# Three edits at the seams of a fused decoder layer: x in row tiles, unsplit products in the first gate/up group, high parts first in the down stage

## The reference

```python
xn = rmsnorm(x, n1g)
z = xn @ w_in                       # 2048 -> conv group, mLSTM q, k, v, o, 8 gate columns
y = concat(conv_group(z), mlstm(z)) # short conv and chunked mLSTM, each with its own norm
x = x + y @ w_out
hn = rmsnorm(x, n2g)
x = x + (silu(hn @ wg) * (hn @ wu)) @ wd
y_out = rmsnorm(x, final_g)
```

## Time and profile before

| | |
|---|---|
| runs | 2497.23, 2492.79, 2495.88 us; median 2495.88 us |
| profiled execution | 2492.38 us, of which the span shown is 2490.3 us |
| PE busy | 2458.9 us (99%) |
| weight loads of PE | 2393.4 us (96%), beside the matmuls |
| DVE, ACT, POOL busy | 1771.7, 895.0, 38.4 us |
| DMA | 325.54 MB, mean 131 GB/s |
| last chain, by engine | PE 94%, DVE 3%, DMA 2%, ACT 1%, issue 1% |

### The profile page before, as it was taken

The page is one execution under the profiler, slowest core; times in us unless marked ns, Lnnn a source line. Parts: engine busy times, 40 slices in busy tenths (PEclk is TensorE's granted clock), DMA queues, the critical chain, the costliest instruction groups (busy, mean ns, idle before and its releaser), DMA issues.

```text
span 2490.3 us, 44310 instructions
## 1 busy us (share of the span) xinstructions
PE 2458.9 (99%) x17632; PEld 2393.4 (96%) x17632; DVE 1771.7 (71%) x2487; ACT 895.0 (36%) x1236; POOL 38.4 (2%) x60
## 2 busy tenths in 40 slices
PE   8999999999999998999999999999999999999998
PEld 8999999999999997999999999999999899999886
DVE  7576575575687668887778777877777866866435
ACT  5212222222133335434343434343444533544313
POOL 0000000000000000000000000000000000000100
PEclk9999999999999999999999999999999999999999
DMA  5433333333235665344343433434333655745722
GB/s 131 99 119 95 84 112 100 89 104 102 86 115 155 186 200 187 111 127 119 102 134 111 128 112 109 127 110 128 100 111 105 250 155 158 266 129 142 274 81 76
DMA packets 458922, 325.54 MB, mean 131 GB/s; under 512 B 14130, under 2 KB 429006, under 8 KB 456368
## 3 DMA queue, kind: packets, MB, share of 16 engines
q1 hardware_dynamic: 403704, 250.29, 34.6%
q10 hardware_dynamic: 51448, 58.42, 7.7%
q0 software_dynamic: 3584, 14.16, 1.5%
HBM read 264.49 MB, written 58.34 MB: 130 GB/s over the span
## 4 chain that ended last, share of the span: by engine, by line
PE 94%; DVE 3%; DMA 2%; ACT 1%; issue 1%; SPq 0%; DVEq 0%; ACTq 0%
PE ps L604 21%; PE ps L844 17%; PE ps L848 17%; PE ps L846 17%; PE ps L607 10%; PE ps L612 3%; PE ps L859 2%; PE ps L952 2%; PE ps L956 2%; PE ps L954 2%; DMA xtok<-in_x_sample_dram 1%; DMA opraw<-hop 0%; PE ps L960 0%; PE ps L961 0%; PE ps L871 0%
## 5 line engine op out<-in xcount | busy, mean ns | idle before, releaser
L844 PE MATMUL ps<-ophi,gw_ring 128*128 128x288 f32 x3248 | 963.2, 297 | 11.7 <-ACT p1c L1291 6.6
L846 PE MATMUL ps<-oplo,gw_ring 128*128 128x288 f32 x3248 | 959.1, 295 | 0.0
L848 PE MATMUL ps<-ophi,gw_ring 128*128 128x288 f32 x3248 | 957.2, 295 | 0.0
L844 PEld LDWEIGHTS ps<-ophi,gw_ring 128*128 128x128 f32 x3248 | 610.1, 188 | 13.6 <-ACT p1c L1291 7.0
L848 PEld LDWEIGHTS ps<-ophi,gw_ring 128*128 128x128 f32 x3248 | 612.7, 189 | 0.0
L846 PEld LDWEIGHTS ps<-oplo,gw_ring 128*128 128x128 f32 x3248 | 610.9, 188 | 0.2
L1017 ACT ACTIVATE whi<-wraw 128x512 fp32r<-128x512 f32 x256 | 160.7, 632 | 597.3 <-PE ps L607 418.5
L604 PE MATMUL ps<-xhi,whi 128*128 128x288 f32 x1536 | 332.6, 298 | 0.0
L607 PE MATMUL ps<-xhi,wlo 128*128 128x288 f32 x1536 | 328.8, 296 | 0.0
L604 PE MATMUL ps<-xlo,whi 128*128 128x288 f32 x1536 | 328.7, 296 | 0.0
L2100 DVE TENSOR_TENSOR gw_ring<-graw_a,gw_ring 128x1024 fp32r<-128x1024 f32 x195 | 238.7, 1224 | 113.4 <-ACT gw_ring L1264 112.8
(11 more groups left out here) (338 smaller groups left out, 2667.6 us busy)
## 6 DMA issues: line engine op xcount, KB each, us to landing
wraw<-in_w_in_dram SPq DMA_DIRECT2D x96, 512.0 KB, 3.9
graw_a<-in_w_ffn_gate_dram SPq DMA_DIRECT2D x59, 512.0 KB, 3.8
graw_a<-in_w_ffn_up_dram SPq DMA_DIRECT2D x59, 512.0 KB, 4.7
graw_a<-in_w_ffn_down_dram SPq DMA_DIRECT2D x42, 512.0 KB, 6.3
wraw<-in_w_out_dram SPq DMA_DIRECT2D x32, 512.0 KB, 4.3
opraw<-hop SPq DMA_DIRECT2D x14, 1152.0 KB, 11.4
graw_b<-in_w_ffn_gate_dram SPq DMA_DIRECT2D x29, 512.0 KB, 3.8
graw_b<-in_w_ffn_up_dram SPq DMA_DIRECT2D x29, 512.0 KB, 4.8
```

The costliest lines, as they stand in the source:

```text
L844: pe.matmul(out, gw_ring[:, slot, 0, k, :], ophi[p][:, k, :], start=start and k == 0, stop=False, skip_group_check=True)
L846: pe.matmul(out, gw_ring[:, slot, 0, k, :], oplo[p][:, k, :], start=False, stop=False, skip_group_check=True)
L848: mm = pe.matmul(out, gw_ring[:, slot, 1, k, :], ophi[p][:, k, :], start=False, stop=k == GK - 1, skip_group_check=True)
```

## The change

Three parts, with nothing else touched.

**x by tiles of tokens.** SP loads six tiles of 96 tokens with whole rows of 8 KB (seven DMAs in the place of fifteen; the last tile is 32 rows of the prompt and 64 of the sample). A unit of work is now half a token tile, n = 2 t + kh with 8 k tiles each: eight transposes, one ACT copy and one DVE subtraction of 768 elements, 12 units in the place of 16. The gate products of one token half run in one piece, the first behind unit 8, the second at the end. The sums of squares are one per tile (three on ACT, three on DVE) and stand behind the units. The first weight quarters are split at n = 5 and 7.

```diff
-    X_PIECES = ((0, 2), (2, 2), (4, 4), (8, 4), (12, 4))
+    XU = 2 * XT
+    KU = KT // 2
-    SQ_ACT = 4
-    IDLE_FIRST, IDLE_X, IDLE_PIECE = 6, 14, (2, 8)
+    SQ_ACT = 3
+    IDLE_FIRST, IDLE_X = 6, 10
...
+            for t in range(XT - 1):
+                sp.dma_start(xtok[:, t, :], xp[t * XTW:(t + 1) * XTW, :]).then_inc(tok_in[t], 16)
+            sp.dma_start(xtok[0:last, XT - 1, :], xp[TP - last:TP, :]).then_inc(tok_in[XT - 1], 16)
+            sp.dma_start(xtok[last:XTW, XT - 1, :], xs[:, :]).then_inc(tok_in[XT - 1], 16)
...
+            def gates(a):
+                pe.wait_ge(x_lo, XU // 2 * (a + 1))
+                for k in range(KT):
+                    for moving in (xhi, xlo):
...
+            for n in range(XU):
+                t, kh = n // 2, n % 2
+                if n >= 3:
+                    pe.wait_ge(x_lo, n - 2)
+                if kh == 0:
+                    pe.wait_ge(tok_in[t], 16 if t < XT - 1 else 32)
+                for i in range(KU):
+                    k = kh * KU + i
+                    mm = pe.transpose(ps[:, 2 + 2 * (n % 3) + i // 4, (i % 4) * XTW:(i % 4 + 1) * XTW],
...
+                if n == XU - 4:
+                    pe.wait_ge(gw_lo, 2)
+                    gates(0)
+            gates(1)
...
+            for n in range(XU):
+                src, own = unit(n)
+                dve.wait_ge(x_hi, n + 1)
+                tt(own(xlo), src, own(xhi).bitcast(F32), ALU.subtract).then_inc(x_lo, 1)
+                if n in (5, 7):
+                    split(1, n // 2 - 2, V_G1)
+            for t in range(SQ_ACT, XT):
+                ins = square(t)
```

```diff
+                    pe.wait_ge(g_lo, p + 1)
+                    pe.wait_ge(op_hi, p - 1)
+                    pe.wait_ge(tok_in[p - 2], 16 * 2)
+                    for k in range(GK):
+                        mm = pe.matmul(ps[:, bank, 0:HT], gw_whole[:, p % 3, 0, k, :], opraw[p][:, k, :],
+                                       start=start and k == 0, stop=k == GK - 1, skip_group_check=True)
+                    mm.then_inc(g_used, 1)
...
             def operand_low(j):
+                dve.wait_ge(g_used, j + 3)
+                dve.wait_ge(op_hi, 5 + 2 * j + 2)
+                for k0, k1 in ((0, 3), (3, 6), (6, GK)):
...
+            whole_ready(0, 0, 3)
+            weight_sum(0, 0, 4)
+            whole_ready(0, 0, 4)
+            norm_start()
+            whole_ready(0, 0, 5)
+            norm_end()
             operand_low(0)
+            upper_gate(0, 0)
+            whole_ready(0, 0, 6)
+            upper_up(0, 0)
             operand_low(1)
             operand_low(2)
             weight_sum(0, 1, 1)
-            group(0, 1, norm=(norm_start, norm_end))
+            group(0, 1, second=True)
```

```diff
+            def first_blocks():
+                pe.wait_ge(dh_hi, 1)
+                pe.wait_ge(d_hi, 1)
+                for part in range(3):
+                    if part == 1:
+                        pe.wait_ge(d_lo, 1)
+                    elif part == 2:
+                        pe.wait_ge(dh_lo, 1)
+                    h, w = (hlo if part == 2 else hhi)[0], (dwlo if part == 1 else dwhi)[0]
+                    for t in range(4):
+                        if part == 0 and t >= 2:
+                            pe.wait_ge((c11_ok, c12_ok)[t - 2], NG1)
...
-                for t in range(5):
+                for t in range(5) if n else (4,):
```

More of the change, by code:

```diff
@@ L320, in hybrid_trunk_step @@
         tile_read = sem("tile_read")
-        tok_in = [sem(f"tok_in{b}") for b in range(len(X_PIECES))]
+        tok_in = [sem(f"tok_in{b}") for b in range(XT)]
         g1_in, gw_in, small_in = sem("g1_in"), sem("gw_in"), sem("small_in")
@@ L876, in group @@
                 bank_a, bank_b, bank_c = BANK_A[u % 3], 1, 4
+                split = lambda p: pe.wait_ge(op_lo, 3 * (p - 2) + 3) if first and u == 1 else None
                 if first and u == 2:
@@ L963, in down_block @@
                 return mm
+            def first_blocks():
[10 more added lines that the diff above has]
+                            pe.wait_ge((c11_ok, c12_ok)[t - 2], NG1)
+                        for k in range(DK4):
+                            pe.matmul(ps[:, DOWN_BANK[t], :], h[:, k, t * P:(t + 1) * P], w[:, k, :],
+                                      start=part == 0 and k == 0, stop=False, skip_group_check=True)
+            first_blocks()
             for n in range(2 * NBD * NCD):
@@ L1024, in _, with square, unit @@
             act.activation(rstd_col[:, 0:1], ident[:, 0:1], ACT.Copy)
-            act.wait_ge(gw_g, 1)
+            act.wait_ge(gw_lo, 1)
             act.activation(gw[:, :, 0:2 * H], gw_raw[:], ACT.Copy).then_inc(gw_hi, 1)
[L1028 to L1042, removed]
-                if k in (KT - 4, KT - 2):
-                    q = (k - (KT - 4)) // 2
-                    hi(1, q, gain=q + 1)
-            for b, t in squares:
-                square(b, t)
+            def square(t):
+                x = xtok[:, t, :]
+                act.activation(x, x, ACT.Square, accum_out=ss_part[:, t, 0:1]).then_inc(ss_ok, 1)
+            def unit(n):
+                t, kh = n // 2, n % 2
+                cols = slice((t % 3) * XTW, (t % 3 + 1) * XTW)
+                own = lambda v: v.rearrange("p (h b k a) t -> p h b k a t", h=2, b=2, a=2)[:, kh, :, :, t // 3, cols]
+                bank = 2 + 2 * (n % 3)
+                return ps[:, bank:bank + 2, 0:4 * XTW].rearrange("p b (k t) -> p b k t", t=XTW), own
+            for n in range(XU):
+                src, own = unit(n)
+                act.wait_ge(xt_done, n + 1)
+                act.activation(own(xhi), src, ACT.Copy).then_inc(x_hi, 1)
+                if n in (5, 7):
+                    hi(1, n // 2 - 2, gain=n // 2 - 1)
+            for t in range(SQ_ACT):
+                square(t)
             hi(1, 2, gain=3)
@@ L1309, in h_store, with group @@
                     act.dma_start(h_t[g - 1 - FS], hf[:, (g - 1) % 2].rearrange("p a t -> p (a t)")).then_inc(hf_st, 16)
-            def group(m, u, first=False, root=False, last=False):
+            def group(m, u, first=False, last=False):
                 g = m * GU + u
@@ L1409, in _ @@
             act.wait_ge(w_used, 4 * I_FFN)
[L1410 removed]
+            for j in range(5):
+                operand_last(j)
+            keep_copy(0, 0, 0, p1c, 2, c11_ok, p1c_ok)
+            whole_copy(0, 0, 3)
+            keep_copy(0, 0, 1, p5c, 4, c22_ok, p5c_ok)
             operand_hi(0)
[L1412 to L1413 removed]
+            whole_copy(0, 0, 4)
             operand_hi(1)
[L1415 to L1417 removed]
+            keep_copy(0, 0, 2, u2c, 2, c12_ok, u2c_ok)
+            whole_copy(0, 0, 5)
             operand_hi(2)
[L1419 to L1420 removed]
+            whole_copy(0, 0, 6)
+            act.wait_ge(r2_in, 1)
+            act.activation(rstd[:], rstd[:], ACT.Sqrt).then_inc(r2_ok, 1)
             operand_hi(3)
[L1422 to L1424 removed]
             operand_hi(4)
[L1426 to L1427 removed]
+            group(0, 1, first=True)
             for w in range(2, GU):
@@ L2192, in pair_sum, with group @@
                 tt(out, a, b, ALU.subtract).then_inc(t_step, 1)
-            def group(m, u, norm=None):
+            def group(m, u, second=False):
                 g = m * GU + u
@@ L2202, in sums @@
                         pair_sum(m if u else m - 1, v, n)
-                upper_up(g - 1, v)
+                if not second:
+                    upper_up(g - 1, v)
                 product_low(m, u, 0)
```

166 lines of the change are left out of this document (52 added, 114 removed).

## The result

| | before | after |
|---|---|---|
| median of 8 runs each, us | 2493.57 | 2501.33 |
| lowest to highest | 2491.82 to 2497.23 | 2499.14 to 2504.22 |
| profiled execution, us | 2492.38 | 2500.83 |
| its span, us | 2490.3 | 2499.1 |

The ratio after/before is 1.003 with a 95% interval of 1.0019 to 1.0040: slower by 7.8 us, where 5.1 less was forecast. It lies outside the range (2485.3 to 2497.3), beyond even the slower rival (2498.3).

The account below looks back on a forecast made before the run. PE, busy 99% of the span, was taken as the bound, so gains come only where it stands still or does less. Terms +2.5 - 4.5 - 3.1 = -5.1 gave 2490.8 on the median, range 2485.3 to 2497.3.

Parts of the forecast that it names:

- Down's exit, -3.1: At the exit of down's block products PE's 3.08 us wait for `hs` goes: -3.1 us, bounds -3.3 and -2.5.
- Entry of gate and up, -4.5: Product 2 starts earlier, unsplit products cost 3.3, then DVE bounds: -4.5 us, bounds -5.0 and -2.0 with the clock down.
- I take it that it stays: Entry of gate and up: the clock stays up through a 2.2 us wait before product 2; otherwise 2.5 us are lost.
- Rival 3: Entry gives nothing: unsplit products cost 3.3, clock falls (2.5), entry 0 to -2, total about -1.6, 2494.3; chance 0.10.
- The x stage, +2.5: From the start to the first input product: that product starts at 36.0 us in the place of 33.5, +2.5.
- the forecast's 36.0: Predicted start of the first input product, in us: W + 13.2 = 34.3, and 1.7 for clock and norm chain.
- the 1.7: x stage: allowance in us for gates at a fallen clock and a later norm chain, which overlap.
- were it gone they would cost that: x stage: the first half of the gates, 4.3 us, is covered by the wait for W, and would otherwise cost that.
- W: x stage: arrival of the first weight half, queued behind all of x, gating the other six units; 21.05 us, before 25.95.
- The rate of x, 300 GB/s: x stage: x loads at 300 GB/s as whole rows, between the 239 on 96 partitions and 407 or 431 on 128.
- rival 1: x comes no faster: W = 25.1, x stage +6.6, total -1.0, 2494.9; chance 0.22.
- Rival 4: Slower: DVE held for weights, W at 26.0, gates' second half at 1.2 GHz: stage +10.0, total +2.4, 2498.3; chance 0.08.

Follow-up runs that it names:

- no_x: The changed kernel with x loaded as before, by pieces of columns; entry of gate and up and down's exit as changed: 2487.26, ratio 0.9975 to before.
- full_gw_first: The changed kernel, but SP waits after the first x tile until the gate weights have landed: 2494.09, ratio interval 0.9992 to 1.0010.
- gw_late_free: The changed kernel with gate-weight operations behind unit 5, without ACT's wait for the gates' first half; executed once, first input product at 44.7 us.
- runs_2k: The changed kernel with each x tile loaded in four pieces of 512 columns, runs of 2 KB: 2492.27, ratio 0.9998 to before.
- no_x_idle: `no_x` with ten unused transposes of the identity on PE before the wait for p1c: 2485.12, ratio 0.9961.
- runs_2k_idle: `runs_2k` with ten unused transposes before p1c: 2490.06; the second such kernel also has the first tile's weights behind unit 11: 2493.19.

## Why the prediction was wrong

**Down's exit, -3.1: right.** The stretch gave 3.2, with the first down block 0.30 us behind the last matmul's start.

**Entry of gate and up, -4.5: right in its mechanism, wrong in the clock.** "I take it that it stays" failed: the wait before product 2 was 2.79 us, not 2.2, and the clock was down for 3.4 us behind it. In the profiled execution it fell a second time behind the longest of DVE's waits, which the forecast had named: 0.6, 1.3 and 2.4 us before products 0, 1 and 3; measured 0.27, 1.30 and 2.12, with 0.32 before product 2. Each fall is 3.4 us at half speed, so 1.7 us. With the clock held by the added transposes, the stage gave 4.2 to 4.5, the forecast's size. Rival 3 had the clock falling and the rest passed on, "entry 0 to -2": this is what after and `no_x` show (-0.6, -2.0). The waits of 2.9 and 3.08 us from which I argued in rows 4 were poor evidence that a wait leaves the clock up; the nearest case, that same place before the change, had it down.

**The x stage, +2.5: wrong, by 15 us.** Two steps failed.
- *Where DVE is held.* I wrote that DVE waits after unit 5 for the first weight half. It stood before unit 0, for a transfer that the change does not touch. The gate weights' DMA is in no term of my sum: I costed the streams that were moved and not what shares the DMA engines with them. Its cost in the profile: the units start at 26.3 and not at 9.5 (`full_gw_first`). Against the forecast's 36.0 the first weight gain comes 12.0 us late (33.08 for 21.05), and the way from it to the last `xlo` takes 2.9 more (11.8 for 8.9); the second gates took the 6.0 us that I had with the 1.7. The 2.9 is a price that I had named, "were it gone they would cost that": with no wait for W left, the first half of the gates (33.9 to 38.2 us) stands in the way, ACT waits 4.17 us for part of it, and DVE 2.65 us for ACT. In `gw_late_free`, without ACT's wait, DVE waits 2.74 us instead for the units that PE turns over behind those gates.
- *The rate of x, 300 GB/s.* It was 236 to 248, rival 1's premise. I concluded from two rows with 2 KB runs "so the run length did not set the rate of x", and then took longer runs as harmless or better. In token tiles with 2 KB runs x comes at 307, my figure; with 8 KB runs at 239. The estimate by the Trainium skill ("SBUF — State Buffer", Door 1: The DMA port swizzle), 327 GB/s at most for a 96-row tile whatever the run, has the 307 under it, and says nothing of the 239.

What remains of the term when both are mended is `runs_2k`: first input product at 38.0, +4.5. My steps against it: W 21.05, measured 22.53; from W to the last `xlo` 8.9, measured 9.5; the gates' second half 4.3, measured 5.9, part of it at 1.2 GHz. The 1.7 I added for clock and norm chain covered the last.

**The rivals.** Rival 1 had the rate right and the time wrong (2494.9). Rival 4, the slower one, had DVE held and the gates slow. Its gates at 1.2 GHz throughout were 8.6 us, where 6.0 were measured with the low clock in part of them, and for the hold it named the weights at 26.0; the hold that came was another, ahead of the units. No case of mine held a transfer on another queue, so 0.04 for slower was too little for a stage that turned a whole load order over.

## What to carry to other kernels

When a stream of DMAs is given longer packets, or fewer and larger DMAs, look at every small transfer that is under way beside it on another queue, and at what stands in order behind its arrival; loading the same rows in pieces of 2 KB removed both the starvation and the lower rate here. Where PE stood for 2.8 us, ten transposes to no use held the clock and were worth 2 us. Of this change the entry and the exit are worth keeping: with the ten transposes they make the fastest version, `no_x_idle`, 2485.12 against 2495.80 for the kernel before in the same series.

## What was not expected of the hardware

- **Packet length and fairness.** Two queues in use at once went packet for packet with 8 KB packets (162 and 162 in 5 us), nearly so with 4 KB (389 and 337). With 2 KB packets the 2048 small ones were through by 8 us, 1010 of them in one us in which x's queue was not full.
- **Size of the pieces and rate.** 96 partitions, whole token tiles: 239 GB/s with 8 KB, 272 with 4 KB, 307 with 2 KB. The kernel before had 239 too, with 1 and 2 KB pieces that walk by columns over all tiles, so the order in DRAM or over partitions, or the size of the DMAs, matters as well; which, was not tried.
- **Transposes and the clock.** The Trainium skill ("TensorE: Matmul & The Clock Gate", Part 4: PE-mode transpose) has transposes not count as PE work in the same way. The runs show both. In the change PE did nothing but transposes from 27.22 us to 32.84, and the clock rose at 31.6 (first two rows below, columns as in rows 4). In `runs_2k` it did nothing else from 8.2 to 20.2 us, with short pauses, and stayed at 1.2 GHz (the rows behind: window, PE busy, count, clock, DMA share, GB/s, and then PE's timeline). The 1.00 of that window is again the column without a record; the first record is the rise at 23.1. The transposes started 0.160 us apart, as they do in the change at 0.50, and not 0.082. The gate products behind them started 0.24 us apart up to 23.0 and then 0.13:
```profile
27.00:31.00 4.00, 3.78 (x24) 3.78 (x25) 2.93 (x5) 2.07 (x3) 0.00 (x0) 0.50 0.00 0
32.00:33.00 1.00, 0.84 (x11) 0.66 (x8) 0.80 (x1) 0.17 (x1) 0.00 (x0) 1.00 0.00 0
```
```profile
8.00:20.50 12.50, 12.10 (x73) 1.00 1.07 296
8.20 10.61 PE L644 MATMUL ps<-ident,xtok 96*128 96x96 f32 x64 [1.84 <-DMA xtok<-in_x_prompt_dram]
...
21.34 0.44 PE L631 MATMUL ps<-xhi,gw 128*128 128x288 f32 x1
23.34 0.29 PE L631 MATMUL ps<-xlo,gw 128*128 128x288 f32 x1
```
  In `no_x_idle` and the two `runs_2k_idle` kernels ten of them inside the wait went with 1.00 behind it. So transposes can raise and hold the clock here, against the page; why those of `runs_2k` did not raise it, no run tells.
- **The two paces** of the out-projection at one clock, 133 and 129.7 ns a matmul, told of above.
